# Layer norms by column thirds between the products, and feed-forward low parts behind the w_down additions

## Chip, cores and metric

The kernel runs on one core of one Trainium2 chip. The metric is device time in microseconds (us) of one launch, the median of several runs. Lower is better.

## The reference, cut to what matters

One inference step of a one-layer hybrid decoder (attention and a state-space branch in parallel). The change touches only its end, for TOK = 1056 tokens (1024 prompt, 32 sample) of 1024 features:

```
h = layer_norm(ALPHA * x + merged @ w_out, ln1_g, ln1_b)
y = layer_norm(ALPHA * h + (silu(h @ w_gate) * (h @ w_up)) @ w_down, ln2_g, ln2_b)
# layer_norm: (x - mean) * rsqrt(var + 1e-5) * g + b, mean and var over the 1024 features
```

Everything is in float32, inputs and outputs.

## The kernel before

Features lie on the 128 partitions (KT = 8 tiles of them), tokens along the free dimension. A product in float32 is made of three products of parts: each operand is split into a high part (fp32r, a rounded copy) and a low part (what is left), and TensorE (PE) adds high·high, high·low and low·high. One "unit" is 128 x 1024 weights; a dense unit makes one tile of 128 output features for all 1056 tokens: 8 tiles x 3 parts x 3 column thirds of CH = 352 tokens, 72 matmuls (`products`, L893). The three thirds of one output lie in three banks of PSUM (bank set 0 is banks 0 to 2, bank set 1 banks 3 to 5).

GpSimd (POOL) splits each unit of weights: `whi` (L736), then `wlo` (L738), into one of two slots, when PE has released that slot (`unit_done`). SyncE (SP) loads the raw weights four units ahead. VectorE (DVE) makes the low parts of activations and all additions, ScalarE (ACT) the high parts, SiLU, squares and roots.

The order of the work, written out by hand on each engine with semaphores:

1. w_out, eight dense units. For each tile DVE adds ALPHA * x (L2477) into `mm` and adds the tile into the running sum `srow` (L2470).
2. Layer norm 1 over all 1056 tokens at once: PE multiplies `srow` by a matrix of ones (L1386), which gives each partition the sum of the features; ACT makes the mean row `murow` (L1830); DVE subtracts it from eight tiles (L2487); ACT squares each tile (L1835) and PE adds the squares, again by the matrix of ones (24 matmuls of 352 columns); ACT takes the root (L1804), DVE the reciprocal over 128 x 1056 (L2496); then per tile DVE scales (L2492), ACT makes the high part `ahi` (L1842), DVE the low part `alo` (L2503).
3. Feed-forward in 11 blocks of 256 hidden features. A block has four dense units (gate and up for j = 0 and 1) and two w_down units. In the code order of PE: block n+1's gate and up, then block n's w_down. DVE: `hidden` makes the products silu(gate) * up into `ff` (L2516) for j = 0 and 1, then both low parts `flo` (L2519); then `down` adds eight outputs into `mm` (`add`, L2417), which frees the bank sets (`res_free0`, `res_free1`) for PE. The last block's w_down stands alone, its additions also make `srow`.
4. Layer norm 2 as in 2, but reciprocal, scaling and bias by thirds; PE turns the result by token (L1469), DVE and ACT each copy half of a tile into one of two buffers `ytok` (L2548, L1868), ACT issues the store.

The loop of DVE in the feed-forward stands in two functions:

```
def hidden(v):
    for j in range(2):
        ...  # product into ff[j]
    for j in range(2):
        ...  # flo[2v+j] = ff[j] - fhi[2v+j]
```

Of the kernel before, what the change touches and what calls it, by code (L numbers as in the profile page):

```python
# [7 lines left out]
F32 = mybir.dt.float32  # L8
# [7 lines left out]
P = 128  # L16
# [80 lines left out]
THIRDS = 96  # L97
LEAD = 6
# [49 lines left out]
def build(nc, a, o, stop=99, debug=None):  # L148
# [5 lines left out]
             "gt_full1": ("rope_full", 32), "tok_stored0": ("x_stored", 32), "tok_stored1": ("prep_full", 48),  # L154
# [3 lines left out]
             "f_hi": ("cw_ready", 2), "f_split": ("st_turned", 2), "bank_read0": ("vecs_ready", 2),  # L158
             "bank_read1": ("qn_hi", 3), "ssq_ready": ("sq_ready", 2), "ssq_used": ("sq_used", 2),
# [7 lines left out]
             "inv_ready": ("e_ready", 32), "n_ready": ("dm_ready", 36)}  # L167
# [257 lines left out]
    srow, sq2, murow, rsrow = ar("srow", [P, TOK]), ar("sq2", [P, 2, TOK]), ar("murow", [P, TOK]), ar("rsrow", [P, TOK])  # L425
    ar = Arena(low)
# [4 lines left out]
    ytok = [Arena(low + 9 * 4096 + b * 4096)(f"ytok{b}", [P, D_MODEL]) for b in range(2)]  # L431
# [19 lines left out]
    def _(sp):  # L451
# [269 lines left out]
        next_weights(2)  # L721

# [139 lines left out]
    def _(pe):  # L862
# [554 lines left out]
        for u in range(4):  # L1417
# [4 lines left out]
        def layer_norm():  # L1422

            pe.wait_ge(sem("srow_ready"), k["srow_ready"].next())
            pe.wait_ge(sem("res_free0"), k["res_free0"].next())
            ones_times(0, srow, True, True).then_inc(sem("mean_ready"), k["mean_ready"].adds(1))
            pe.wait_ge(sem("res_free1"), k["res_free1"].next())
            for e in range(KT):
                pe.wait_ge(sem("ssq_ready"), k["ssq_ready"].next())
                ones_times(1, sq2[:, e % 2], e == 0, e == KT - 1).then_inc(sem("ssq_used"), k["ssq_used"].adds(1))  # L1430

        layer_norm()


# [14 lines left out]
        gate_and_up(tile_split)  # L1449
# [5 lines left out]
        down(0)  # L1455
        layer_norm()

        thirds_done = 0
        for i in range(9):
            n = P if i < 8 else NS  # L1460
            if i == 0:
                for b in range(2):
                    pe.wait_ge(sem(f"res_free{b}"), k[f"res_free{b}"].next())
            pe.wait_ge(sem(f"bank_read{i % 2}"), k[f"bank_read{i % 2}"].held(2))
            while thirds_done * CH < i * P + n:
                pe.wait_ge(sem("affine_ready"), k["affine_ready"].next(KT))
                thirds_done += 1
            for e in range(KT):
                last = pe.transpose(ps[0:n, 2 * (i % 2) + e // 4, e % 4 * P:(e % 4 + 1) * P], mm[:, e, i * P:i * P + n], ident)  # L1469
            last.then_inc(sem("tok_turned"), k["tok_turned"].adds(1))  # L1470


    @block.scalar
    def _(act):
# [353 lines left out]
        def layer_norm():  # L1828
            act.wait_ge(sem("mean_ready"), k["mean_ready"].next())
            act.activation(thirds(murow[:, :]), out3(0), ACT.Copy, scale=1.0 / D_MODEL).then_inc(sem("res_free0"), k["res_free0"].adds(1))  # L1830
            for e in range(KT):
                act.wait_ge(sem("centred"), k["centred"].next())
                if e >= 2:
                    act.wait_ge(sem("ssq_used"), k["ssq_used"].next())
                act.activation(sq2[:, e % 2], mm[:, e], ACT.Square).then_inc(sem("ssq_ready"), k["ssq_ready"].adds(1))  # L1835
            act.wait_ge(sem("ssq_used"), k["ssq_used"].next(2))
            root(1, rsrow, D_MODEL)
        k["res_free1"].n += 6 * 4 + KT // 2
        layer_norm()
        for e in range(KT):  # L1840
            act.wait_ge(sem("scaled"), k["scaled"].next())
            act.activation(ahi[:, e], mm[:, e], ACT.Identity, bias=vecs[:, V_L1B + e:V_L1B + e + 1]).then_inc(sem("g_hi"), k["g_hi"].adds(1))  # L1842
# [9 lines left out]
        k["unit_done"].n = TOTAL_UNITS - 6 * NF  # L1852
        for j in range(2):
            gate(0, j)
# [6 lines left out]
        k["res_free1"].n += 4  # L1861
        layer_norm()
        def by_token(tiles):
            for i in tiles:
                n = P if i < 8 else NS
                act.wait_ge(sem("tok_turned"), k["tok_turned"].next())
                act.wait_ge(sem(f"tok_stored{i % 2}"), k[f"tok_stored{i % 2}"].same())
                act.activation(ytok[i % 2][0:n, 0:512], ps[0:n, 2 * (i % 2), :], ACT.Copy).then_inc(sem(f"bank_read{i % 2}"), k[f"bank_read{i % 2}"].adds(1))  # L1868
                k[f"bank_read{i % 2}"].n += 1
                act.wait_ge(sem(f"bank_read{i % 2}"), k[f"bank_read{i % 2}"].same())  # L1870
                dst = o["y_prompt"][0, i * P:i * P + n, :] if i < 8 else o["y_sample"].rearrange("b t d -> (b t) d")
                act.dma_start(dst, ytok[i % 2][0:n, :]).then_inc(sem(f"tok_stored{i % 2}"), k[f"tok_stored{i % 2}"].adds(16))
# [709 lines left out]
```

## Time and profile before

| | |
|---|---|
| median of 3 runs | 3094.28 us (3092.59 to 3104.74) |
| profiled execution, its own time | 3096.15 us |
| its span, first to last instruction | 3094.3 us |
| PE busy | 2908.1 us (94%) |
| DVE, ACT, POOL busy | 1556.8, 748.1, 1027.7 us |
| mean granted clock of PE | 0.966 |

The span is what the trace shows; 1.85 us of the execution's own time lie outside it. Times in the trace are counted from the start of the span. The granted clock is a share of PE's full speed: 1.00 is 2.4 GHz and 0.50 is 1.2 GHz. Ends of matmuls are modelled, so distances between starts are read rather than durations.

### The profile page before, as it was taken

What the parts mean: (1) busy time and instruction counts of PE and PEld (TensorE: products, weight loads), DVE (VectorE), ACT (ScalarE), POOL (GpSimd) and SP (SyncE); (2) the same over time, 40 slices, a digit from 0 to 9 for tenths busy, and PEclk for the clock granted to TensorE, in tenths of its full rate; (3) what the DMA queues carried; (4) which work ended last, traced back from release to release, by engine and by line L of the source; (5) the groups of instructions that cost most, each with busy time, mean ns of one, the idle gap of its engine ahead of it and who ended that gap; (6) DMA issues with size and microseconds to landing.
All of it is one profiled execution on the core that took longest, in us unless ns stands there. A gap on an engine that the chain in (4) does not pass through costs nothing.

```text
span 3094.3 us, 45505 instructions
## 1 busy us (share of the span) xinstructions
PE 2908.1 (94%) x18732; PEld 2591.8 (84%) x18732; DVE 1556.8 (50%) x2123; ACT 748.1 (24%) x1143; POOL 1027.7 (33%) x586
## 2 busy tenths in 40 slices
PE   7799999999999999999999688999799999999996
PEld 7789999999989975555776588999599999999995
DVE  2765787756474736554444567663512222222226
ACT  1211212435363624554332100100200000000003
POOL 3443333423232404544002032444133333333330
PEclk9899999999999979999999899999899999999998
DMA  4154234656564552223233323343011111111101
GB/s 134 54 162 138 83 100 136 161 158 162 165 171 132 155 148 62 65 82 139 101 147 138 112 91 119 126 153 103 22 48 42 45 45 42 42 48 42 42 21 56
DMA packets 314164, 308.84 MB, mean 100 GB/s; under 512 B 31813, under 2 KB 272714, under 8 KB 311498
## 3 DMA queue, kind: packets, MB, share of 16 engines
q1 hardware_dynamic: 250808, 190.24, 21.8%
q10 hardware_dynamic: 59594, 78.22, 7.3%
q0 software_dynamic: 3584, 37.75, 3.2%
q8 instruction: 143, 2.34, 0.3%
q14 instruction: 35, 0.29, 0.0%
HBM read 227.96 MB, written 78.20 MB: 99 GB/s over the span
## 4 chain that ended last, share of the span: by engine, by line
PE 69%; DVE 12%; issue 9%; POOL 5%; ACT 2%; DMA 2%; SPq 1%; ACTq 0%; POOLq 0%; DVEq 0%
PE ps L893 42%; PE ps L1053 10%; POOL pr L839 4%; PE ps L1386 2%; PE ps L1329 2%; PE ps L1289 2%; PE ps L1302 2%; DVE cv L2030 2%; DVE flo L2519 1%; PE ps L1306 1%; PE ps L1132 1%; PE ps L1086 1%; PE ps L1090 1%; PE ps L964 1%; PE ps L1079 1%
## 5 line engine op out<-in xcount | busy, mean ns | idle before, releaser
L736 POOL TENSOR_TENSOR whi<-raw,cst 128x1024 fp32r<-128x1024 f32 x160 | 309.0, 1931 | 1242.7 <-PE ps L893 1099.9
L893 PE MATMUL ps<-ahi,whi 128*128 128x352 f32 x1824 | 399.1, 327 | 54.7 <-DVE alo L2390 22.4
L738 POOL TENSOR_TENSOR wlo<-raw,whi 128x1024 fp32r<-128x1024 f32 x160 | 440.7, 2755 | 12.6
L893 PE MATMUL ps<-alo,whi 128*128 128x352 f32 x1824 | 397.3, 326 | 0.0
L893 PE MATMUL ps<-ahi,wlo 128*128 128x352 f32 x1824 | 393.7, 324 | 0.0
L893 PEld LDWEIGHTS ps<-ahi,whi 128*128 128x128 f32 x1824 | 311.7, 190 | 62.9 <-issue 40.0
L893 PEld LDWEIGHTS ps<-ahi,wlo 128*128 128x128 f32 x1824 | 313.8, 190 | 0.0
L893 PEld LDWEIGHTS ps<-alo,whi 128*128 128x128 f32 x1824 | 312.8, 189 | 0.0
L1053 PE MATMUL ps<-xhi,whi 128*128 128x352 f32 x768 | 256.0, 333 | 0.0
L1053 PE MATMUL ps<-xhi,wlo 128*128 128x352 f32 x768 | 248.0, 323 | 0.0
L1053 PE MATMUL ps<-xlo,whi 128*128 128x352 f32 x768 | 247.9, 323 | 0.0
L2417 DVE TENSOR_TENSOR mm<-ps,mm 128x1056 f32<-128x1056 f32 x112 | 139.7, 1256 | 151.2 <-PE ps L893 149.8
L839 POOL TENSOR_TENSOR pr<-pr,rowinv 128x384 f32<-128x384 f32 (+7 forms) x128 | 145.4, 1146 | 204.0 <-DVE rowinv L2235 203.0
L1183 PE MATMUL ps<-kb,qb 96*128 96x512 f32 (+3 forms) x384 | 161.2, 538 | 10.9 <-ACT pr L1704 8.4
L893 PE MATMUL ps<-xhi,whi 128*128 128x352 f32 x720 | 158.5, 329 | 6.7 <-ACT xraw L1570 4.4
L893 PE MATMUL ps<-xlo,whi 128*128 128x352 f32 x720 | 157.0, 326 | 0.0
L2228 DVE TENSOR_REDUCE rowmax<-ps 128x1 f32<-128x384 f32 (+7 forms) x128 | 97.0, 758 | 117.7 <-PE ps L1185 115.9
L893 PE MATMUL ps<-xhi,wlo 128*128 128x352 f32 x720 | 155.4, 324 | 0.0
L1183 PEld LDWEIGHTS ps<-kb,qb 96*128 96x128 f32 x384 | 65.5, 198 | 105.5 <-issue 77.0
L1053 PEld LDWEIGHTS ps<-xhi,whi 128*128 128x128 f32 x768 | 144.3, 188 | 7.9 <-issue 5.5
L1053 PEld LDWEIGHTS ps<-xlo,whi 128*128 128x128 f32 x768 | 144.4, 188 | 0.0
L1053 PEld LDWEIGHTS ps<-xhi,wlo 128*128 128x128 f32 x768 | 144.4, 188 | 0.0
(329 smaller groups left out, 5016.2 us busy)
## 6 DMA issues: line engine op xcount, KB each, us to landing
raw<-in_w_in SPq DMA_DIRECT2D x61, 512.0 KB, 5.1
s_a<-d_acum SPq DMA_DIRECT2D x32, 512.0 KB, 7.1
d_xbc<-so ACTq DMA_DIRECT2D x24, 528.0 KB, 2.7
gt<-d_g SPq DMA_DIRECT2D x24, 528.0 KB, 3.6
raw<-in_w_ffn_gate SPq DMA_DIRECT2D x22, 512.0 KB, 3.8
raw<-in_w_ffn_up SPq DMA_DIRECT2D x22, 512.0 KB, 3.8
raw<-in_w_ffn_down SPq DMA_DIRECT2D x22, 512.0 KB, 3.5
d_z<-zo ACTq DMA_DIRECT2D x16, 528.0 KB, 5.2
```

Of the source, the lines that this page charges most:

```text
L736: pool.tensor_tensor(whi[s][:, :], raw[:, u], ones[:, 0:1].broadcast_to([P, UNIT]), ALU.mult).then_inc(sem("unit_hi"), k["unit_hi"].adds(1))
L738: pool.tensor_tensor(wlo[s][:, :], raw[:, u], whi[s][:, :].bitcast(F32), ALU.subtract).then_inc(sem("unit_split"), k["unit_split"].adds(1))
L839: pool.tensor_tensor(pr[G][i][:, :], pr[G][i][:, :], rowinv[:, n:n + 1].broadcast_to([P, length]), ALU.mult).then_inc(sem("n_ready"), k["n ...
L893: last = pe.matmul(ps[0:m, 3 * b + c, 0:width], w(j), x[:, j, at:at + width], start=i == 0, stop=i == n - 1)
L1053: last = pe.matmul(ps[:, c, 0:CH], w[u % SPLIT][:, j * P:(j + 1) * P], x[:, j, c * CH:(c + 1) * CH], start=i == 0, stop=i == 3 * KT - 1)
L1183: pe.matmul(ps[:, first_bank + c // 512, 0:w], qb[pp][h][:, q * P:(q + 1) * P], kb[pp][h][:, c:c + w], start=True, stop=True)
L1289: last = pe.transpose(ps[:, 4 + i % 3, r * P:(r + 1) * P], src, ident)
L1302: pe.matmul(half(c, s), qcur[b][:, j, :], kvt[:, j, 4 * g:4 * g + 4, :].rearrange("p r n -> p (r n)"), start=j == 0, stop=False)
L1329: last = pe.matmul(ps[64 * s:64 * s + 64, 7, 0:KL], prt[:, i, 64 * s:64 * s + 64], kvb[b][:, 8 * c + 4 * s + i % 4, :], start=i == 0, stop ...
L1386: last = pe.matmul(ps[:, 3 * b + c, 0:width], ones, src[:, at:at + width], start=start, stop=stop_)
L2228: dve.tensor_reduce(rowmax[:, n:n + 1], src, AX, ALU.max).then_inc(step.sem, step.adds(1))
L2417: dve.tensor_tensor(thirds(mm[:, e]), out3(b), thirds(mm[:, e]), ALU.add).then_inc(sem(f"res_free{b}"), k[f"res_free{b}"].adds(1))
```

## The change

**Feed-forward.** In `hidden` the low part of j = 0 is made right behind the product of j = 0. The low part of j = 1 is made after the eight additions of `down` (and, at the end of the loop, the last w_down on PE still waits for it).

**Layer norms by thirds.** The sum, mean, centring, squares, root, factor, scaling and splitting are done for each third of 352 tokens. On PE they stand between products: the last two w_out units and the first two gate and up units go by thirds (`unit_third`), and the last w_down goes by thirds over the eight outputs (`last_down`), each part in the next of six banks.

**Statistics by token.** The sum of squares is no longer a product with the matrix of ones as the stationary operand. For each run of TS = 88 tokens the squares are the stationary operand (128 x 88) and one column of ones moves, so the sums of 88 tokens land in one column (32 matmuls a third, `square_sums`). The root and the reciprocal are then of 88 x 4 values, and `spread` brings them back to a row on all partitions (4 matmuls a third with the 88 x 88 identity moving); ACT copies that row to SBUF (`factor_row`). Centring and squaring take four tiles in one instruction (128 x 4 x 352).

**Output.** Nine buffers `ytok` in place of two, three pairs of banks in place of two, and SP issues the stores.

```diff
+        def square_sums(c, n):
+            pe.wait_ge(sem("row_read"), k["row_read"].held())
+            pe.wait_ge(sem("squared"), k["squared"].next(2))
+            for t in range(CH // TS):
+                for e in range(KT):
+                    last = pe.matmul(ps[0:TS, 7, CH + t:CH + t + 1], sqb[n][:, e, t * TS:(t + 1) * TS], ones[:, 0:1], start=e == 0, stop=e == KT - 1)
+            last.then_inc(sem("sums_done"), k["sums_done"].adds(1))
+        def spread(c):
+            pe.wait_ge(sem("inverted"), k["inverted"].next())
+            for t in range(CH // TS):
+                at = c * (CH // TS) + t
+                last = pe.matmul(ps[:, 7, t * TS:(t + 1) * TS], inv[0:TS, at:at + 1].broadcast_to([TS, P]), ident[0:TS, 0:TS], start=True, stop=True)
+            last.then_inc(sem("row_ready"), k["row_ready"].adds(1))
# PE, from w_out to the feed-forward
-        for u in range(4, 8):
-            dense(u, u % 2, ahi, alo, KT)
-        layer_norm()
+        unit_third(6, 0)
+        unit_third(7, 0)
+        unit_third(6, 1)
+        mean(0)
+        unit_third(7, 1)
+        unit_third(6, 2)
+        square_sums(0, 0)
+        mean(1)
+        unit_third(7, 2)
+        spread(0)
+        mean(2)
+        square_sums(1, 0)
+        unit_third(0, 0, "g_split")
+        spread(1)
+        unit_third(1, 0)
+        square_sums(2, 0)
+        unit_third(0, 1, "g_split")
+        spread(2)
+        unit_third(1, 1)
+        unit_third(0, 2, "g_split")
+        unit_third(1, 2)
+        for u in range(2, 4):
             dense(u, u % 2, ahi, alo, KT)
# PE, the end
+        pe.wait_ge(sem("f_split"), k["f_split"].next(2))
+        for b in range(2):
+            pe.wait_ge(sem(f"res_free{b}"), k[f"res_free{b}"].next())
+        last_down(0, 0, 8)
+        last_down(1, 0, 3)
+        mean(0)
+        last_down(1, 3, 8)
+        last_down(2, 0, 2)
+        mean(1)
+        last_down(2, 2, 3)
+        square_sums(0, 1)
+        last_down(2, 3, 6)
+        spread(0)
+        last_down(2, 6, 8)
+        mean(2)
+        square_sums(1, 1)
+        by_token(0)
+        by_token(1)
+        spread(1)
+        square_sums(2, 1)
+        spread(2)
+        for i in range(2, 9):
+            by_token(i)
# DVE, norm 1
+        last_residual(0)
+        centre(0)
+        last_residual(1)
+        inverse(0)
+        centre(1)
+        last_residual(2)
...
+        split_third(0)
+        inverse(1)
+        centre(2)
+        split_third(1)
+        inverse(2)
+        split_third(2)
# DVE, feed-forward
                 dve.tensor_tensor(thirds(ff[j][:, :]), out3(1), thirds(fg[j]), ALU.mult).then_inc(sem("res_free1"), k["res_free1"].adds(1))
-            for j in range(2):
-                dve.wait_ge(sem("f_hi"), k["f_hi"].next())
-                dve.tensor_tensor(flo[:, 2 * v + j], ff[j][:, :], fhi[:, 2 * v + j].bitcast(F32), ALU.subtract).then_inc(sem("f_split"), k["f_split"].adds(1))
+                if j == 0:
+                    low_part(v, 0)
...
             for v in range(2):
                 hidden(1 - v)
                 down()
+                low_part(1 - v, 1)
# DVE, the end: per part one addition into mm and one into srow
+        last_down(0, 0, 8)
+        last_down(1, 0, 3)
+        centre(0)
+        last_down(1, 3, 8)
+        last_down(2, 0, 2)
+        centre(1)
+        last_down(2, 2, 3)
+        inverse(0)
+        last_down(2, 3, 8)
+        scale_third(0)
+        centre(2)
+        inverse(1)
+        right_half(0)
+        right_half(1)
+        scale_third(1)
+        inverse(2)
+        right_half(2)
+        scale_third(2)
+        for i in range(3, 9):
+            right_half(i)
```

`last_residual(c)` is the ALPHA * x addition of tiles 6 and 7 for one third and their additions into `srow`; `centre(c)` two subtractions of 128 x 4 x 352; `split_third(c)` eight scalings and eight low parts of 352 columns, waiting for ACT's high parts; `low_part(v, j)` one `flo`. On ACT: mean row, squares, root, factor row, high parts or bias, for each third in turn.

## Rows read from the trace of the kernel before

**Rows 1.** The page, part 1: engine, busy time, share of the span, instructions.

```profile
PE 2908.1 (94%) x18732; PEld 2591.8 (84%) x18732; DVE 1556.8 (50%) x2123; ACT 748.1 (24%) x1143; POOL 1027.7 (33%) x586
```

**Rows 2.** Busy time of each engine by stretch, clock, DMA (norm 1, feed-forward, end).

```profile
core 0: us, PE busy (x) PEld busy (x) DVE busy (x) ACT busy (x) POOL busy (x), PEclk, DMA share, GB/s
2160.54:2252.95 92.41, 70.52 (x344) 60.16 (x343) 54.02 (x39) 22.61 (x20) 20.15 (x8) 0.87 0.12 35
2252.95:3009.68 756.73, 732.00 (x4465) 727.94 (x4464) 181.76 (x123) 46.10 (x43) 275.80 (x124) 0.99 0.14 42
3009.68:3094.30 84.62, 56.95 (x271) 47.37 (x269) 55.30 (x61) 29.45 (x44) 4.29 (x2) 0.86 0.13 52
```

**Rows 3.** Chain that ended last, around norm 1: start, length, what.

```profile
2186.88 3.90 PE ps L1386 x6
...
2194.40 17.05 PE ps L1386 x48
...
2212.65 6.76 DVE rsrow L2496
...
2238.12 24.00 PE ps L893 x147
```

**Rows 4.** Chain that ended last, at the end of the kernel.

```profile
3042.82 16.10 PE ps L1386 x48
...
3081.60 2.64 DMA out_y_prompt<-ytok
```

**Rows 5.** Waits from 2240 us on: who for whom, total, times, longest.

```profile
PE ps L893 <- DVE mm L2417: 21.3, 10, 2.2
```

**Rows 6.** PE in order of time, norm 1's gate unit, a w_down start: start, length, idle.

```profile
2233.20 0.75 PE L893 MATMUL ps<-ahi,whi 128*128 128x352 f32 x3 [0.75 <-DVE alo L2503]
2233.79 0.65 PE L893 MATMUL ps<-alo,whi 128*128 128x352 f32 x3
...
2987.15 0.65 PE L893 MATMUL ps<-flo,whi 128*128 128x352 f32 x3
2987.64 0.64 PE L893 MATMUL ps<-fhi,wlo 128*128 128x352 f32 x3
2990.44 0.75 PE L893 MATMUL ps<-fhi,whi 128*128 128x352 f32 x3 [2.17 <-DVE mm L2417]
...
2992.37 1.08 PE L893 MATMUL ps<-fhi,whi 128*128 128x352 f32 x3
2993.25 1.08 PE L893 MATMUL ps<-flo,whi 128*128 128x352 f32 x3
```

**Rows 7.** Line L2519, the low parts: least, median, greatest ns.

```profile
L2519 DVE TENSOR_TENSOR flo<-srow,fhi x11: 1719/1785/1879, 2277.4 to 2983.8; 128x1056 fp32r<-128x1056 f32 x11
L2519 DVE TENSOR_TENSOR flo<-rsrow,fhi x11: 3450/3455/3458, 2279.2 to 2985.5; 128x1056 fp32r<-128x1056 f32 x11
```

**Rows 8.** DVE and POOL in order of time at that w_down start.

```profile
2982.66 1.26 DVE L2516 TENSOR_TENSOR rsrow<-ps,sq 128x1056 f32<-128x1056 f32 x1 [21.89 <-PE ps L893]
...
2989.13 2.42 DVE L2417 TENSOR_TENSOR mm<-ps,mm 128x1056 f32<-128x1056 f32 x2
2982.61 1.89 POOL L736 TENSOR_TENSOR whi<-raw,cst 128x1024 fp32r<-128x1024 f32 x1 [7.26 <-PE ps L893]
2984.59 3.30 POOL L738 TENSOR_TENSOR wlo<-raw,whi 128x1024 fp32r<-128x1024 f32 x1
```

**Rows 9.** DVE and ACT in order of time, in the two norms.

```profile
2191.88 9.44 DVE L2487 TENSOR_TENSOR mm<-mm,murow 128x1056 f32<-128x1056 f32 x8 [5.06 <-ACT murow L1830]
3062.51 4.06 DVE L2492 SCALAR_TENSOR_TENSOR mm<-mm,vecs,rsrow 128x352 f32<-128x352 f32 x8
2198.36 1.08 ACT L1835 ACTIVATE sq<-mm 128x1056 f32<-128x1056 f32 x1 [2.93 <-PE ps L1386]
3063.12 4.06 ACT L1878 ACTIVATE mm<-mm,vecs 128x352 f32<-128x352 f32 x8 [3.04 <-DVE mm L2492]
```

**Rows 10.** PE in order of time, elsewhere: float32 matmuls with few moving columns.

```profile
1128.33 1.02 PE L1121 MATMUL ps<-s_e,s_it 128*64 128x4 f32 x16
...
1722.08 0.39 PE L1335 MATMUL ps<-rowsum,cst 128*128 128x5 f32 x2
1723.43 5.52 PE L1367 MATMUL ps<-cst,oseq 128*128 128x64 f32 x32 [0.97 <-DVE oseq L2339]
```

**Rows 11.** Busy time by stretch again: small matmuls, and turning by token.

```profile
1122.00:1127.00 5.00, 5.00 (x33) 4.10 (x32) 1.51 (x5) 1.16 (x2) 0.00 (x0) 0.50 0.86 225
3082.00:3084.00 2.00, 2.00 (x11) 2.00 (x10) 0.00 (x0) 0.60 (x1) 0.00 (x0) 0.50 0.81 322
3090.00:3092.00 2.00, 0.00 (x0) 0.00 (x0) 0.68 (x1) 0.59 (x1) 0.00 (x0) 1.00 0.99 395
```

More of the change, by code:

```diff
@@ L97 @@
 THIRDS = 96
+TS = 88
 LEAD = 6
@@ L1432, in _, with third, unit_third @@
-        layer_norm()
+        def third(c):
+            return slice(c * CH, (c + 1) * CH)
+        def unit_third(u, c, ready=None):
+            s = u % SPLIT
+            if c == 0:
+                pe.wait_ge(sem("unit_split"), k["unit_split"].next())
+                pe.wait_ge(sem(f"res_free{s}"), k[f"res_free{s}"].next())
+            for i in range(3 * KT):
+                j, part = divmod(i, 3)
+                if ready and part == 0:
+                    pe.wait_ge(sem(ready), k[ready].next())
+                w, x = ((whi, ahi), (whi, alo), (wlo, ahi))[part]
+                last = pe.matmul(ps[:, 3 * s + c, 0:CH], w[s][:, j * P:(j + 1) * P], x[:, j, third(c)], start=i == 0, stop=i == 3 * KT - 1)
+            last.then_inc(sem("unit_done" if c == 2 else "third_ok"), k["unit_done" if c == 2 else "third_ok"].adds(1))
@@ new lines, in mean @@
+        def mean(c):
+            pe.wait_ge(sem("srow_ready"), k["srow_ready"].next())
+            pe.wait_ge(sem("mu_ready"), k["mu_ready"].held())
+            pe.matmul(ps[:, 6, 0:CH], ones, srow[:, third(c)], start=True, stop=True).then_inc(sem("mean_ready"), k["mean_ready"].adds(1))
+        def square_sums(c, n):
[5 more added lines that the diff above has]
+            last.then_inc(sem("sums_done"), k["sums_done"].adds(1))
@@ L1838, in _, with squares @@
[L1838 to L1842, printed above, removed]
+            act.activation(murow[:, third(c)], ps[:, 6, 0:CH], ACT.Copy, scale=1.0 / D_MODEL).then_inc(sem("mu_ready"), k["mu_ready"].adds(1))
+        def squares(c, n):
+            for h in range(2):
+                act.wait_ge(sem("centred"), k["centred"].next())
+                if h == 0:
+                    act.wait_ge(sem("sums_done"), k["sums_done"].same())
+                act.activation(sqb[n][:, 4 * h:4 * h + 4, :], mm[:, 4 * h:4 * h + 4, third(c)], ACT.Square).then_inc(sem("squared"), k["squared"].adds(1))
@@ new lines, in high_parts @@
+        def high_parts(c):
+            for e in range(KT):
+                act.wait_ge(sem("scaled"), k["scaled"].next())
+                act.activation(ahi[:, e, third(c)], mm[:, e, third(c)], ACT.Identity, bias=vecs[:, V_L1B + e:V_L1B + e + 1]).then_inc(sem("g_hi"), k["g_hi"].adds(1))
+        mean_row(0)
+        squares(0, 0)
+        root_of(0)
+        mean_row(1)
+        squares(1, 0)
+        factor_row(0)
+        mean_row(2)
+        high_parts(0)
+        root_of(1)
+        factor_row(1)
@@ new lines, in centre, with inverse @@
+        def centre(c):
+            dve.wait_ge(sem("mu_ready"), k["mu_ready"].next())
+            dve.wait_ge(sem("srow_ready"), k["srow_ready"].same())
+            for h in range(2):
+                part = mm[:, 4 * h:4 * h + 4, third(c)]
+                dve.tensor_tensor(part, part, murow[:, third(c)].unsqueeze(1).broadcast_to([P, 4, CH]), ALU.subtract).then_inc(sem("centred"), k["centred"].adds(1))
+        def inverse(c):
+            n = CH // TS
+            dve.wait_ge(sem("rooted"), k["rooted"].next())
+            dve.reciprocal(inv[0:TS, c * n:(c + 1) * n], stat[0:TS, c * n:(c + 1) * n]).then_inc(sem("inverted"), k["inverted"].adds(1))
```

237 lines of the change are left out of this document (142 added, 95 removed).

## The prediction

> **What bounds the kernel.** I read the page's first part, then busy time by stretch, then the chain of waits and the timelines inside each stretch. PE is busy for 94% of the span [rows 1], so a stage is worth what PE loses in it. I cut the touched end of the kernel at three places of PE: the end of w_out unit 5 (2160.54), the end of the second feed-forward unit (2252.95), the start of the last w_down (3009.68). The stretches last 92.4, 756.7 and 84.6 us [rows 2].
>
> A product costs PE 0.485 us for three matmuls, start to start [rows 6]: 0.1616 each, 11.635 for a unit. The first stretch holds four units, 46.5 us, so norm 1 costs 45.9. The second holds 62 units (2, then 10 x 6), 721.4 us; 35.3 are lost. The third holds two, 23.3; norm 2 and the output cost 61.3.
>
> The chain in norm 1 [rows 3] is serial: sum on PE, 17.05 us of squares against ones, 6.76 of reciprocal, then scaling and splitting; PE runs freely only from 2238.12. Norm 2 repeats it [rows 4] and ends in stores. The loss in the feed-forward is PE waiting ten times for the first w_down addition, 21.3 us in all [rows 5]. After a wait of 2.17 us two groups run at 0.88 instead of 0.485 us [rows 6], half the clock; four such groups are 1.6 us. 2.1 + 1.6 = 3.7, and the stretch gives 3.53 per block.
>
> **Feed-forward low parts.** The first w_down addition starts at 2989.13 because two low parts, 1.78 and 3.45 us [rows 7], lie between it and the product at 2982.66 [rows 8]. Now only the product stands ahead: it ends at 2983.9. PE ends output 0 eighteen matmuls (2.91 us) after 2982.3, at 2985.2; the addition takes 1.26 and frees the bank set at 2986.5. PE wants it at 2988.1, so 1.6 us remain to spare. The low part of j = 0 moves into the 11.6 us before the second product; that of j = 1 follows the eighth addition, some 20 us before the next product. Both are hidden by PE's units, and without that cover would cost what they cost today. All 35.3 us go: **-35.3**. The tall low part is tall because of POOL: it starts under L738, which itself takes 3.30 then [rows 8].
>
> That row is what the Trainium skill states (SBUF — State Buffer, the section with the engine and AXI sides): a VectorE instruction with two SBUF inputs and a GpSimd one shut each other out for the whole instruction. The trace agrees, 3.45 us for what takes 1.2 otherwise.
>
> **Prices of the new operations.** *Square sums*, 32 matmuls, and the trace records a float32 matmul as two instructions: 64. Not seen in this shape. Lower bound from 64 stationary columns, 60 ns each (L1121, at half the clock), upper from 128 columns, 125 ns (L1335, start to start 0.13) [rows 10]: 3.8 to 8.0 us. 88 columns lie between, 84 ns in proportion: 5.4. *Spread*, 8 instructions with 128 stationary columns: L1367's 0.17 gives 1.3. *Mean*, three times a third of the 24 squares matmuls, 16.10/24 = 0.67 us [rows 4], at the full clock. *Centring*, 4 x 352 columns: 9.44/8 = 1.18 for 1056 [rows 9], so 1.57 each, 3.2 a third, unless the repeated row costs more (bound 2.5 each). *Squares* on ACT 1.08 x 4/3 = 1.4 each. *Small DVE or ACT operations* of 352 columns 0.51 [rows 9]; one that waits for the other's end 0.55. Root and inverse of 88 x 4: under 0.4 together with the handover. Three reciprocals of 2.3 and one of 6.76 go.
>
> The Trainium skill (TensorE: Matmul & The Clock Gate, the section on LDWEIGHTS) prices a load by its columns at P/1.2 ns. For 88 that is 73 ns; its estimate for a third's square sums would be 4.7 us. The 125 ns of 128 columns here is 107 and a little, so the trace agrees.
>
> **Norm 1**, from T = 0 at the end of unit 5. Unit 6 by thirds reaches 3.9. Unit 7 needs POOL's split of its slot, which starts at 0 and takes 1.89 + 3.30 [rows 8]: it starts at 5.4 (before, 11.6 us of unit 6 hid this) and its third ends at 9.3. Next third of unit 6: 13.2; mean: 13.9; third of 7, last third of 6: 21.6. Meanwhile centring ends at 17.7 and squares at 19.1, both in time. Square sums 27.0, mean 27.7, last third of unit 7 31.6, spread 32.9. Here DVE is late: centring of third 1 to 31.5, then four operations of the last residual to 33.8; mean(2) ends 34.5. Square sums 39.9. The gate unit follows DVE's splitting (16 operations, 8.2 us) to 43.8; spread 45.1, third of the up unit 48.9, square sums 54.4, gate third 58.2, spread 59.5, up third 63.4. The last gate third waits for DVE (scaling from 60.0, last low part 68.5): 69.0; last up third 72.9; the next unit waits for its split until 73.7.
>
> Two additions. The split of the up unit starts at 31.6, just where DVE's two additions into `srow` of third 2 have two SBUF inputs; by the 3.45 row one waits for L736 or L738: 0 to 3 us, I take 2. Clock: a wait of 2.17 costs 1.6 us behind it, one of 0.75 costs 0.1 [rows 6]; here are waits of 1.6 and 1 to 4, and PE stood at 0.50 under small matmuls though busy 5.00 of 5.00 us [rows 11], so the square sums may go with half the clock. Between none and five drops, 0 to 8; I take 2.5. Sum 78.2 against 92.4: **-14.2**. With square sums 3.8 and no additions 70 (-22); with 8.0 and 4 of additions 85.5 (-7).
>
> **The end**, from T = 0 at the start of the last w_down. A new wait: PE needs the last addition of the block before, and behind it on DVE the low part of j = 1: 1.3 + 1.8 (its start lies where the shorter one of rows 7 lies against POOL), so PE starts at 3.1; everything of that w_down stands behind this wait. From there DVE is slower than PE: a part costs PE 0.97, DVE two operations, 1.1. Sum of third 0 at 12.9; mean(1) waits 3.4 us for DVE and ends at 25.2; square sums 31.6; sum of third 2 at 39.1; scaling of third 0 43.2; square sums 45.2, tiles 0 and 1 47.3; spread 48.6; square sums 54.6; spread 56.6; tile 2 57.6. DVE's half of tile 2 (58.4) stands ahead of scaling of third 2, whose bias ends at 63.0. Six tiles are then turned; copies end at 67.8. Their stores, 2.75 MB at 0.395 MB per us [rows 11], outlast them: 72.2. Slow clock as in the turning now (0.50, [rows 11]), in the mean and the first parts: +4.3 (0 to 6). 76.5 against 84.6: **-8.1**; bounds -15 (3.8, no slow clock) and -2 (8.0, slow). Nine buffers remove the present waits for stores of 2.64 [rows 4]; SP is idle then, so its issue costs nothing.
>
> **Sum.** -35.3 - 14.2 - 8.1 = -57.6. The profiled execution's 3096.15 becomes 3038.5. Its time stands 1.87 above the median, 3094.28, so the forecast is **3037 us**.
>
> **Rivals.**
> - *The statistics are dear* (0.20): square sums near 8 us, or PE at half clock behind them. For: 125 ns with 128 columns and 0.50 under small matmuls. Against: the loads have 88 columns and dense work lies between. All bounds at the dear end: -35.3 - 7 - 2 = -44; with more drops -36. 3050 to 3058.
> - *Everything fits* (0.15): short square sums, no drop, no lock: -35.3 - 22 - 15 = -72: 3022.
> - *The feed-forward stall stays* (0.05), the change not doing what it says: another operation of DVE or ACT holds the bank set, and 1.6 us to spare are too few. Against: no such operation is in the queue. -22: 3072.
> - *Slower than before* (0.02): one mechanism, the price of a one-column float32 matmul. Each us more of square sums costs 3 us in each norm, so the gain is gone at 5.4 + 57.6/6 = 15 us, 235 ns an instruction, and 0.5% is lost at 17.6, 275 ns; at 18, 3112. Nothing in rows 10 is above 172.
>
> The forecast itself, 3029 to 3046, has 0.55; 0.03 lies elsewhere. The range from the bounds is 3022 to 3052: it leaves out half of the dear case, the stall and the slow one. Half a percent is 15.5 us, about what a measurement of this kernel can tell from no change: only the slow rival and part of the unnamed rest come near. Faster 0.95, same 0.03, slower 0.02.
>
> **What would show it.** No idle time of PE before the third output of w_down, and the middle stretch 721 to 723 us. First stretch 70 to 85, square sums 3.8 to 8.0 each, the clock behind them at 1.00. In the end, PE's first matmul of the last w_down about 3 us late, then DVE without pause. I am wrong if the clock is 0.50 for most of norm 1, if the 128 x 4 x 352 centring takes over 2.5 us, or if a stall comes back in the blocks.

## The result, and the profile after

The changed kernel takes 3063.22 us (median of 4 runs, 3053.06 to 3065.72) against 3094.7 for the kernel before on the same chip: a ratio of 0.9873, 95% interval 0.9853 to 0.9893. It is 31 us faster, where the forecast said 57; 3063 lies 11 us above the wide range of 3022 to 3052. The profiled execution took 3062.58 us, its span is 3060.8. The first part of the page, for [rows 1]:

```profile
PE 2922.0 (95%) x19068; PEld 2621.2 (86%) x19068; DVE 1562.5 (51%) x2190; ACT 753.1 (25%) x1169; POOL 1028.8 (34%) x586
```

Busy time by stretch of the changed kernel, cut where [rows 2] are cut (end of w_out unit 5, end of the second feed-forward unit, start of the last w_down); the number before the DMA share is the granted clock:

```profile
core 0: us, PE busy (x) PEld busy (x) DVE busy (x) ACT busy (x) POOL busy (x), PEclk, DMA share, GB/s
2169.23:2253.14 83.91, 78.54 (x510) 75.38 (x508) 53.17 (x75) 27.47 (x41) 18.84 (x9) 0.86 0.11 32
2253.14:2974.26 721.12, 721.12 (x4464) 720.83 (x4464) 184.53 (x127) 46.06 (x43) 274.72 (x124) 1.00 0.14 44
2974.26:3060.80 86.54, 71.86 (x439) 69.15 (x438) 53.29 (x89) 29.31 (x49) 5.14 (x2) 0.73 0.13 51
```

| stretch | before | forecast | after | after minus forecast |
|---|---|---|---|---|
| up to the end of unit 5 | 2160.54 | 2160.54 | 2169.23 | +8.7 |
| norm 1 | 92.4 | 78.2 | 83.9 | +5.7 |
| feed-forward | 756.7 | 721.4 | 721.1 | -0.3 |
| the end | 84.6 | 76.5 | 86.5 | +10.0 |

The last column sums to 24.1, and 3038.5 + 24.1 = 3062.6, the profiled execution's own time: nothing is missing. The feed-forward came as forecast, both norms are too long, and 8.7 us were lost where no line was changed. PE is busier than before in both norms (78.5 us against 70.5 in [rows 2], 71.9 against 57.0) and its clock at the end is 0.73 against 0.86: it waits less than before, and it is slow.

**Norm 1.** PE of the changed kernel in order of time (start, length, idle before): the mean, the square sums of the first third, the mean behind them, a product, then the square sums of the other two thirds.

```profile
2174.59 0.43 PE L1447 MATMUL ps<-ahi,whi 128*128 128x352 f32 x1 [1.59 <-POOL wlo L751]
2182.39 0.76 PE L1454 MATMUL ps<-srow,cst 128*128 128x352 f32 x2
...
2190.67 5.85 PE L1462 MATMUL ps<-cst,yz 128*88 128x1 f32 x64
2196.39 1.52 PE L1454 MATMUL ps<-srow,cst 128*128 128x352 f32 x2
2197.19 1.01 PE L1447 MATMUL ps<-ahi,whi 128*128 128x352 f32 x1
...
2206.60 7.83 PE L1462 MATMUL ps<-cst,yz 128*88 128x1 f32 x64
2214.29 0.64 PE L1447 MATMUL ps<-ahi,whi 128*128 128x352 f32 x1
```

The same stretches with the clock (the number behind the instruction count): sums, mean, product third; sums, product third; the last product third behind sums.

```profile
core 0: us, PE busy (x), PEclk, DMA share, GB/s
2190.78:2196.47 5.69, 5.69 (x66) 0.85 0.01 3
2196.47:2197.90 1.43, 1.43 (x4) 0.50 0.81 231
2197.94:2203.46 5.52, 5.52 (x26) 0.67 0.11 33
2206.70:2214.40 7.70, 7.70 (x66) 0.61 0.25 70
2214.40:2220.40 6.00, 6.00 (x28) 0.64 0.00 0
2230.90:2237.10 6.20, 6.20 (x27) 0.61 0.00 1
```

Up to the first square sums the ledger of the prediction holds to a tenth of a microsecond (with T = 0 at 2169.2: unit 7 at 5.4, mean at 13.2, square sums at 21.5). PE then goes from the full clock to the half clock while it is busy 5.69 of 5.69 us, and it stays low into the product behind. The three sums take 5.69 + 7.70 + 5.8 = 19.2 us (the third, at a clock of 0.83, isn't shown) where 16.2 stood in the ledger, and the three product thirds behind them 5.52 + 6.00 + 6.20 = 17.7 where 11.6 stood: 9.1 us, of a total of 10.2 over the ledger without its two additions. Those additions were 4.5, so 5.7 are left.

The clash of DVE and POOL that the prediction added is there, at the place it named. DVE of the changed kernel at the split of the up unit, which POOL starts at 2203.57:

```profile
2204.08 1.76 DVE L2636 TENSOR_TENSOR srow<-srow,mm 128x352 f32<-128x352 f32 x1
2205.77 3.16 DVE L2651 SCALAR_TENSOR_TENSOR mm<-mm,vecs,rsrow 128x352 f32<-128x352 f32 x2
```

The same operations take 0.52 and 0.58 each when POOL is quiet.

**The end.** PE of the changed kernel in order of time:

```profile
2977.47 0.66 PE L1530 MATMUL ps<-fhi,whi 128*128 128x352 f32 x1 [3.21 <-DVE flo L2685]
...
3000.26 1.50 PE L1454 MATMUL ps<-srow,cst 128*128 128x352 f32 x2 [1.99 <-DVE srow L2732]
...
3003.32 6.46 PE L1462 MATMUL ps<-cst,sqb 128*88 128x1 f32 x64
...
3019.81 7.93 PE L1462 MATMUL ps<-cst,sqb 128*88 128x1 f32 x59
3027.61 3.62 PE L1547 MATMUL ps<-cst,mm 128*128 128x128 f32 x16
...
3032.63 7.98 PE L1462 MATMUL ps<-cst,sqb 128*88 128x1 f32 x64 [0.55 <-ACT rsrow L1950]
3041.17 2.01 PE L1470 MATMUL ps<-cst,inv 88*128 88x88 f32 x8 [0.56 <-DVE inv L2648]
```

The wait of 3.1 us at the last w_down is 3.21. The sums take 6.5, 8.1 and 8.0 us (the second starts at 3019.47; its row above lacks its first instructions), 22.6 against 16.2. The first parts go at a clock of 0.50, the parts behind the first sums at 0.56, the turning at 0.65, and the last spread takes 2.01 us where the others take 1.02. The last copy ends at 3056.4, that is 82.1 after the start of the last w_down where the ledger had 67.8. The kernel ends 4.4 us behind it, and the ledger had 4.4 there too (72.2 less 67.8): the stores kept their share, and all else came later.

### The profile page after: what moved, and what is told of

It reads as the page before. It is cut to its first block, busy times and chain, and to the rows that moved or that the text cites. A ratio compares the mean times of both kernels' runs of the same rounds, so it can differ in the third digit from the quotient of the medians.

```text
span 3060.8 us, 46298 instructions
## 1 busy us (share of the span) xinstructions
PE 2922.0 (95%) x19068; PEld 2621.2 (86%) x19068; DVE 1562.5 (51%) x2190; ACT 753.1 (25%) x1169; POOL 1028.8 (34%) x586
## 4 chain that ended last, share of the span: by engine, by line
PE 68%; DVE 11%; issue 10%; POOL 5%; ACT 2%; DMA 2%; SPq 1%; ACTq 0%; POOLq 0%; DVEq 0%
PE ps L906 39%; PE ps L1066 10%; POOL pr L852 4%; DVE cv L2168 3%; PE ps L1342 2%; PE ps L1302 2%; PE ps L1315 2%; PE ps L1462 1%; PE ps L1447 1%; PE ps L1319 1%; DVE cv L2162 1%; PE ps L1145 1%; PE ps L1099 1%; DVE cv L2170 1%; DMA gt<-d_z 1%
## 5 line engine op out<-in xcount | busy, mean ns | idle before, releaser
L751 POOL TENSOR_TENSOR wlo<-raw,whi 128x1024 fp32r<-128x1024 f32 x160 | 438.8, 2742 | 12.6
L906 PE MATMUL ps<-ahi,whi 128*128 128x352 f32 x1728 | 377.1, 326 | 37.2 <-DVE alo L2528 21.8
L906 PE MATMUL ps<-alo,whi 128*128 128x352 f32 x1728 | 376.2, 326 | 0.0
L906 PE MATMUL ps<-ahi,wlo 128*128 128x352 f32 x1728 | 373.4, 325 | 0.0
L906 PEld LDWEIGHTS ps<-ahi,whi 128*128 128x128 f32 x1728 | 295.5, 190 | 42.8 <-issue 22.0
L906 PEld LDWEIGHTS ps<-ahi,wlo 128*128 128x128 f32 x1728 | 297.5, 190 | 0.0
L906 PEld LDWEIGHTS ps<-alo,whi 128*128 128x128 f32 x1728 | 296.1, 189 | 0.0
L2555 DVE TENSOR_TENSOR mm<-ps,mm 128x1056 f32<-128x1056 f32 x104 | 130.5, 1257 | 164.9 <-PE ps L906 164.8
```

The source lines that it names most:

```text
L751: pool.tensor_tensor(wlo[s][:, :], raw[:, u], whi[s][:, :].bitcast(F32), ALU.subtract).then_inc(sem("unit_split"), k["unit_split"].adds(1))
L906: last = pe.matmul(ps[0:m, 3 * b + c, 0:width], w(j), x[:, j, at:at + width], start=i == 0, stop=i == n - 1)
L2555: dve.tensor_tensor(thirds(mm[:, e]), out3(b), thirds(mm[:, e]), ALU.add).then_inc(sem(f"res_free{b}"), k[f"res_free{b}"].adds(1))
```

## The experiments

All kernels stand beside runs of the kernel before on the same chip. In the stages, "head" is the end of w_out unit 5; they are read from the starts of POOL's splits, which moves the cuts by up to 0.3 us against the windows above. Each row is one profiled execution; the median is of all runs.

| kernel | median, us | ratio, 95% | head | norm 1 | feed-forward | end |
|---|---|---|---|---|---|---|
| low parts only | 3073.7 | 0.9915 (0.9892 to 0.9939) | 2161.1 | 92.3 | 725.5 | 90.6 |
| old end | 3064.45 | 0.9888 (0.9867 to 0.9910) | 2160.5 | 84.2 | 720.9 | 92.0 |
| norms only | 3086.59 | 0.9948 (0.9929 to 0.9967) | 2166.1 | 84.2 | 750.8 | 82.6 |
| changed kernel again | 3058.83 | 0.9854 (0.9835 to 0.9874) | 2168.8 | 85.7 | 720.9 | 85.1 |
| sums twice | 3114.17 | 1.0048 (1.0031 to 1.0065) | 2163.0 | 111.9 | 726.0 | 110.9 |
| sums by ones | 3045.55 | 0.9821 (0.9805 to 0.9838) | 2167.0 | 78.5 | 724.6 | 73.9 |
| sums between | 3076.76 | 0.9922 (0.9897 to 0.9947) | 2166.0 | 101.0 | 720.9 | 86.5 |
| low part mid | 3057.56 | 0.9866 (0.9850 to 0.9883) | 2167.8 | 84.1 | 720.9 | 82.8 |
| ones and mid | 3044.62 | 0.9819 (0.9800 to 0.9838) | 2169.3 | 78.6 | 725.0 | 72.4 |
| kernel before again | 3103.86, one run | | 2169.2 | 91.1 | 757.2 | 84.5 |
| changed kernel once more | 3059.81, one run | | 2166.5 | 84.1 | 720.9 | 86.5 |

The kernel before had medians of 3102.81 us beside the first four kernels, 3101.21 beside the next four and 3100.47 beside the last three.

### The parts alone

**Low parts only.** The kernel before with the feed-forward part of the change; norms and output as before.

```diff
+        def low_part(v, j):
+            dve.wait_ge(sem("f_hi"), k["f_hi"].next())
+            dve.tensor_tensor(flo[:, 2 * v + j], ff[j][:, :], fhi[:, 2 * v + j].bitcast(F32), ALU.subtract).then_inc(sem("f_split"), k["f_split"].adds(1))
-            for j in range(2):
-                dve.wait_ge(sem("f_hi"), k["f_hi"].next())
-                dve.tensor_tensor(flo[:, 2 * v + j], ...)
+                if j == 0:
+                    low_part(v, 0)
...
+        low_part(0, 1)
...
+                low_part(1 - v, 1)
```

> The kernel before with the feed-forward low parts moved and nothing else. By the traces of before and after, the stretch of the blocks falls from 756.7 to 721.1 us (-35.6), norm 1 and the end stay at 92.4 and 84.6 us. Theory A (the unchanged part ahead of norm 1 varies from execution to execution by some 9 us, and the changed kernel's profiled execution was a long one): median near 3059, and the end of w_out unit 5 lies anywhere between 2160 and 2170 us in the trace. Theory B (the 8.7 us belong to the changed program's norm code): unit 5 ends at 2160.5 again and the median is 3059. Rival C (the low part behind the additions makes a stall elsewhere): more than 3065.

**Old end.** The changed kernel with the last w_down, layer norm 2 and the output of the kernel before (one `ps` bank set after the other, squares against ones, two `ytok`, stores from ACT). PE's part of the edit:

```diff
-        last_down(0, 0, 8)
-        last_down(1, 0, 3)
-        mean(0)
...
-        for i in range(2, 9):
-            by_token(i)
+        down(0)
+        layer_norm()
```

> The changed kernel with its end (last w_down, layer norm 2, output) as it was before: low parts moved, norm 1 by thirds, norm 2 over all tokens. By the traces: norm 1 stretch 83.9 us, blocks 721.1, end 84.6, which is 1.9 us less than the end by thirds. Expected 1 to 3 us faster than the changed kernel of the same chip, about 3051 if unit 5 ends at 2160 and 3060 if it ends at 2169. Rival: the end by thirds is worth the 8 us that were forecast and the profiled execution only hid it; then this kernel is 8 us slower than the changed one.

**Norms only.** The changed kernel with both low parts back ahead of the additions.

```diff
-                if j == 0:
-                    low_part(v, 0)
+            for j in range(2):
+                low_part(v, j)
...
-                low_part(1 - v, 1)
```

> The changed kernel with both low parts ahead of the w_down additions, as before: norms by thirds alone. By the traces: norm 1 stretch 83.9 (-8.5), blocks 756.7, end: the new wait for the low part of j = 1 goes, some 1.5 us of 86.5, so about 85 (+0.4). Expected -8 without the 8.7 us ahead of norm 1: 3087; if these belong to the program (theory B): 3095; if they vary (theory A): either, from run to run.

**The changed kernel again**, on the same chip.

> The changed kernel once more, for its profile and its times on the same chip. Theory A: unit 5 ends anywhere between 2160 and 2170 us, and the three stretches behind it are again 83.9, 721.1 and 86.5 us within 2 us each; the median lies between 3053 and 3063. Theory B: unit 5 ends at 2169 again.

Waits of PE in the blocks (total, times, longest): the kernel before beside its stalls of [rows 5], the norms-only kernel and the low-parts-only kernel, one fence each. "issue" is time in which PE waited for nothing that the profile shows.

```profile
PE ps L893 <- issue: 3.4, 4, 1.2
```

```profile
PE ps L906 <- DVE mm L2555: 21.3, 10, 2.2
```

```profile
PE ps L893 <- issue: 3.5, 4, 1.1
```

The norms-only kernel has the ten stalls of [rows 5] and no gaps: 750.8 - 720.9 = 29.9 us is what the stalls and the slow groups behind them cost, and it is all that the move of the low parts gives back. The clock doesn't fall behind each stall. Here are the 6 us of PE behind the second and the third stall of the kernel before:

```profile
2402.80:2408.80 6.00, 6.00 (x37) 1.00 0.11 33
2475.80:2481.80 6.00, 6.00 (x28) 0.72 0.10 29
```

Five of its ten stalls are like the second line, with nine matmuls fewer or some 1.5 us lost, and five like the first; in the norms-only kernel it is four and six. Waits of 21.3 us and five times 1.5 make 28.8 of the 35.3 lost in the kernel before; waits of 21.3 and four times 1.5 make 27.3 of the 29.9 in the norms-only kernel, and its other 2.6 us were not traced.

The low-parts-only kernel has no stall in the blocks but four small gaps in which PE waited for nothing shown, 0.7 to 1.1 us, 141 us apart, which is one pass of the loop (12 units, five passes): one at each jump back. Its blocks take 725.5, so the gaps and what stands behind them cost 4.6. The kernel before has both. The gaps go with the program and not with the low parts: both executions of the kernel before have them, and so do "sums twice" (4.2 us in four), "sums by ones" (2.7) and "ones and mid", two of which have the changed kernel's loop unchanged, while the changed kernel has none in three executions. What in a program makes them was not tried.

At the end, low parts only costs 90.6 - 84.6 = 6.0 us and old end 7.4: the new wait of 3.2 is in both traces, with a slow clock behind it and no gain beside them. So "low parts only" missed its expectation: 3073.7 is 29.1 below the kernel before on its chip, where a median near 3059 was expected. "Old end" missed too: 1 to 3 us less than the changed kernel was expected, and it takes 5.6 more (3064.45 against 3058.83 on the same chip; the ends are 92.0 and 85.1). The end by thirds is worth something then, but only against an old end that has the new wait as well. The norm-1 part is worth 8.2 us in "old end" and in "norms only" alike.

### The square sums

**Sums twice.** Each third's 32 one-column matmuls are made twice over.

```diff
-            for t in range(CH // TS):
+            for t in [*range(CH // TS)] * 2:
```

> The changed kernel with each square sum made twice, 64 one-column matmuls a third in place of 32 (the second writes the same sums). It measures what they cost on the path. By the prediction's ledger each us more in a third's sums costs 3 us in each norm: with 5.4 to 8 us a third, 32 to 48 us more in all. If DVE's chain hid part of them, less than 25; if the clock stays at half in the doubled run (8 us for 64 instructions), up to 50.

PE in order of time, the first two doubled sums:

```profile
2184.45 15.15 PE L1462 MATMUL ps<-cst,yz 128*88 128x1 f32 x128
...
2208.61 18.36 PE L1462 MATMUL ps<-cst,yz 128*88 128x1 f32 x128
```

Norm 1 grows by 26 to 28 us and the end by 24.4 to 25.8, 52 in all and some 9 us a third for 64 more instructions, each of which costs about 0.14 us. That is more than the 32 to 48 expected. The sums themselves grew by 9.3 to 10.5 us a third, so the prediction's slope (3 us in each norm for each us of a third's sums) roughly holds. So does its slower rival, which put the end of the gain at 15 us a third and a loss of 0.5% at 17.6: here are 15 to 18 us, and 3114.17 is 0.5% above the kernel before.

**Sums by ones.** By thirds as in the changed kernel, but the sum of squares is again a product with the matrix of ones (16 instructions with 352 moving columns), root and reciprocal over 128 x 352, and no spread.

```diff
-            for t in range(CH // TS):
-                for e in range(KT):
-                    last = pe.matmul(ps[0:TS, 7, CH + t:CH + t + 1], sqb[n][:, e, t * TS:(t + 1) * TS], ones[:, 0:1], start=e == 0, stop=e == KT - 1)
+            for e in range(KT):
+                last = pe.matmul(ps[:, 7, 0:CH], ones, sqb[n][:, e, :], start=e == 0, stop=e == KT - 1)
...
-        spread(0)
...
-            dve.reciprocal(inv[0:TS, c * n:(c + 1) * n], stat[0:TS, c * n:(c + 1) * n])...
+            dve.reciprocal(rsrow[:, third(c)], rsrow[:, third(c)])...
```

> The changed kernel with the square sums of both norms made as before, by the matrix of ones with 352 columns moving, still by thirds: 8 matmuls a third in place of 32 with one column, no spread, no factor row; DVE takes the reciprocal over 128 x 352 (2.35 us a third). Theory A (the one-column matmuls let the clock fall to half, inside them and in the products behind): a third's sums cost 8 x 0.59 = 4.7 us in place of 5.7 to 8.2, the clock of the products behind them is 1.00, and both stretches shrink: norm 1 from 84 to about 77 us, the end from 86 to about 78, some 12 us in all. Theory B (what makes the norms long is DVE's chain): the three reciprocals add 7 us to each stretch, and the kernel is as slow as the changed one or slower.

The three stretches of this kernel, and two of its sums in order of time:

```profile
2167.00:2245.50 78.50, 67.33 (x343) 57.45 (x342) 59.05 (x75) 27.06 (x38) 20.41 (x9) 0.96 0.12 34
2245.50:2970.10 724.60, 721.87 (x4464) 720.43 (x4463) 184.33 (x127) 46.06 (x43) 275.10 (x124) 1.00 0.15 44
2970.10:3044.00 73.90, 54.84 (x270) 46.06 (x270) 58.82 (x89) 28.94 (x46) 5.16 (x2) 0.87 0.15 59
```

```profile
2188.41 4.89 PE L1461 MATMUL ps<-yz,cst 128*128 128x352 f32 x16
...
2204.07 1.54 PE L1454 MATMUL ps<-srow,cst 128*128 128x352 f32 x2 [6.34 <-DVE srow L2614]
2205.40 7.00 PE L1461 MATMUL ps<-yz,cst 128*128 128x352 f32 x16
```

The same columns as above (clock behind the instruction count) for the first of these sums:

```profile
2188.30:2193.10 4.80, 4.80 (x18) 1.00 0.02 3
```

This is the kernel that settles the cause. Sums that move 352 columns leave the clock at 0.96 in norm 1 and 0.87 at the end, where one-column sums gave 0.86 and 0.73; the stretches are 78.5 and 73.9, the first what the forecast had for the changed kernel, the second less. DVE's three reciprocals and a wait of 6.3 us for DVE are in that price, and it still wins 5.4 to 7.2 and 11.2 to 12.6 us over the changed kernel's executions. The sums by ones also fall to half clock once, behind the wait of 6.34 (7.00 us instead of 4.89). The statistics by token are thus a loss here; the thirds are the gain. What of the one-column matmuls it is (one moving column in place of 352, or 88 stationary columns in place of 128) these runs don't separate, and the kernel without spread and factor row also has fewer handovers; what those gave back was not measured apart.

**Sums between.** The one-column matmuls of each third stand one or two behind every product matmul of the next third of products, so that they never form a row.

```diff
+        def with_sums(u, t, ready, c, n):
...
+            for i in range(3 * KT):
...
+                last = pe.matmul(ps[:, 3 * s + t, 0:CH], w[s][:, j * P:(j + 1) * P], x[:, j, third(t)], start=i == 0, stop=i == 3 * KT - 1)
+                for q in range(i * 32 // 24, (i + 1) * 32 // 24):
+                    r, e = divmod(q, KT)
+                    sums = pe.matmul(ps[0:TS, 7, CH + r:CH + r + 1], sqb[n][:, e, r * TS:(r + 1) * TS], ones[:, 0:1], start=e == 0, stop=e == KT - 1)
...
-        square_sums(0, 0)
         mean(1)
-        unit_third(7, 2)
+        with_sums(7, 2, None, 0, 0)
```

> The changed kernel with one thing moved: in norm 1 the 32 one-column matmuls of a third are not issued in a row but one or two behind each of the 24 matmuls of the product third beside them. Same instructions, same count. Theory A (a row of 64 one-column instructions lets the clock fall): the clock stays at 1.00 through norm 1, 24 products with 32 sums take 3.9 + at most 5.7 us in place of 5.7 + 5.6 or 7.7 + 6.0, so the PE time of the three pairs falls by some 6 to 8 us; DVE gets the sums later, so the stretch falls by 2 to 6 us from 84. Theory B (the clock falls for the gaps of PE, not for the one-column matmuls): clock as now, stretch as now or longer by the later sums.

Norm 1's first mixed stretch by clock, and PE where it falls:

```profile
2187.00:2194.70 7.70, 7.70 (x67) 1.00 0.15 42
2194.70:2215.00 20.30, 11.84 (x53) 0.50 0.12 36
```

```profile
2194.28 0.24 PE L1472 MATMUL ps<-cst,yz 128*88 128x1 f32 x2
2194.38 0.41 PE L1469 MATMUL ps<-alo,whi 128*128 128x352 f32 x1
2194.63 0.25 PE L1472 MATMUL ps<-cst,yz 128*88 128x1 f32 x2
2194.74 0.59 PE L1469 MATMUL ps<-ahi,wlo 128*128 128x352 f32 x1
2195.12 0.65 PE L1472 MATMUL ps<-cst,yz 128*88 128x1 f32 x4
```

The clock falls in the middle of the mixture, with PE busy all the time, and stays at 0.50. Waits stand in that second stretch, but the next mixture has none and is as slow:

```profile
2215.00:2225.40 10.40, 10.40 (x53) 0.50 0.01 2
```

Norm 1 takes 101.0 us, 15 to 17 more than with the sums in a row. The expectation had the row of 64 as the cause and a shorter stretch; it isn't the row that does it: small matmuls pull the clock down when they are spread among products too, and then the products beside them pay. Part of the 101.0 is a wait of 6.2 us of the last mean for DVE, which the later order brings; its share was not measured apart.

### The low part at the last w_down

**Low part mid.** The second low part between the third and the fourth of the eight additions.

```diff
                 add(e, e % 2)
+                if e == 2:
+                    low_part(v, 1)
...
-                low_part(1 - v, 1)
```

> The changed kernel with the low part of j = 1 between the third and the fourth w_down addition in place of behind the eighth. There DVE has 1.65 us to spare for 1.26 us and POOL is idle. Theory A (the low part behind the additions makes PE start the last w_down 3.2 us late and at half the clock): the blocks stay at 721 us, the last w_down starts at once, and the end falls from 85 to 86.5 us by 3 to 5. Rival (the wait for the last additions holds PE as long anyway, or DVE sets the end): the end falls by 1.5 us at most.

PE at its last w_down:

```profile
2974.34 0.40 PE L1530 MATMUL ps<-fhi,whi 128*128 128x352 f32 x1 [1.55 <-DVE mm L2555]
2974.57 0.32 PE L1530 MATMUL ps<-flo,whi 128*128 128x352 f32 x1
```

The wait is 1.55 us instead of 3.21, now for the last addition, and the matmuls behind it go at full clock (0.16 us from one to the next). The end takes 82.8 us, 2.3 to 3.7 less, and the blocks are as short as before. "Norms only", with the low parts ahead, has 82.6. In the whole time the gain doesn't show: the ratio is 0.9866 where the changed kernel has 0.9854 and 0.9873.

**Ones and mid.** Both in one kernel.

> Token sums by the ones matrix as in the kernel before, but by column thirds, and the second low part of w_down between the third and the fourth addition. If the small square-sum matmuls and the low part's place are two separate costs, they add: against the changed kernel -5.7 us in norm 1 and some -12 us at the end from the sums, some -3 us at the end from the low part's place. The end then measures about 71 us, norm 1's stretch 78.5, the blocks 720.9 or 724.6, and the whole 3038 to 3045 us. If instead the wait of 3.2 us at the last w_down is hidden behind DVE's other work once the sums are cheap, the end stays at 74 us and the whole at 3044.

3044.62 against 3045.55 of "sums by ones": the two can't be told apart, though the end measures 72.4 against 73.9. At the end 1.5 of the 3 us arrive; where the others go was not traced. Both are faster than either kernel of this case: their eight runs take 3040.69 to 3046.97 us, the nine of the changed kernel 3052.64 to 3065.72.

### The 8.7 us ahead of norm 1

**The kernel before again**, unchanged:

> The kernel before, unchanged, profiled once more. If the 5 to 9 us that the changed kernels lose ahead of norm 1 come from how DVE and POOL happen to fall against each other in one execution, the end of w_out's unit 5 comes here anywhere between 2160 and 2169 us; if they belong to the program, it comes at 2160.5 as in the first profile, and the four small gaps at the loop's jump back are there again.

**The changed kernel once more**:

> The changed kernel, unchanged, profiled a third time. If the loss ahead of norm 1 belongs to the program, the end of w_out's unit 5 comes at 2168.8 to 2169.2 us as twice before and the blocks take 720.9 us; if it is chance, elsewhere between 2160 and 2169.

The kernel before has its unit 5 end at 2160.54 in one profile and at 2169.2 in the other; the changed kernel at 2169.2, 2168.8 and 2166.5. The same program gives both, so it is no cost of the change. The two profiles of the kernel before may come from different chips, but on one chip the first four kernels of the table, edited only behind this point, lie between 2160.5 and 2168.8, and seven runs of the kernel before on one chip differ by 8 to 10 us. It is chance of the execution as far as these runs show. DVE by line from 510 to 582 us (the convolution, 15 operations of the same shape), first the kernel before in its first profile, then in its second:

```profile
L2030 DVE SCALAR_TENSOR_TENSOR cv<-xraw,cw,cv 128x1024 f32<-128x1024 f32 x15 | 19.3, 1285 | 0.5
```

```profile
L2030 DVE SCALAR_TENSOR_TENSOR cv<-xraw,cw,cv 128x1024 f32<-128x1024 f32 x15 | 23.1, 1543 | 0.5
L2024 DVE TENSOR_SCALAR cv<-xraw,cw 128x1024 f32<-128x1024 f32 x5 | 7.8, 1563 | 0.0
```

PE in that second profile, in order of time:

```profile
570.36 1.91 PE L1145 MATMUL ps<-cst,ccol 128*27 128x128 f32 x8 [4.78 <-DVE cv L2032]
```

In the first profile PE is busy all of the 71.5 us from 510 to 581.5, at the full clock. In the second it is busy for 65.7 of them: two of DVE's 15 operations start just behind a split of POOL and take 3.47 and 2.97 us, the convolution comes late, PE waits 4.78 us and goes at half the clock for a while. One such meeting, DVE and then POOL:

```profile
519.68 3.47 DVE L2030 SCALAR_TENSOR_TENSOR cv<-xraw,cw,cv 128x1024 f32<-128x1024 f32 x1
519.67 2.40 POOL L738 TENSOR_TENSOR wlo<-raw,whi 128x1024 fp32r<-128x1024 f32 x1
```

POOL's splits date the loss: the split at 551.35 in the first profile comes 0.9 us later in the second, the one at 580.24 comes 9.8 later, the one at 2089.83 comes 8.7 later. The changed kernel's first profile shows 23.1, 1542 for the same line, so the two are the same case.

## Why the prediction was right and wrong

**Right: the feed-forward, -35.3.** Measured -35.6, with PE busy 721.12 of 721.12 us; the 1.6 us to spare at the first addition held in all ten blocks. But the account of it was wrong in part, and the sum came right by luck. All 35.3 were given to the stall, as 2.1 + 1.6 a block; "norms only" shows 29.9 for it. The slow clock follows only half of the stalls, and [rows 6] shows one of that half. The rest goes with four issue gaps of 3.4 us in all, and the changed program happens to have none. They stand in the same view of waits as [rows 5], unpriced.

**Right: the places.** The wait of 3.1 at the last w_down (3.21), the clash of DVE and POOL in norm 1, the centring of 1.57 an instruction (3.16 for two), the spread of 1.3 (0.87 to 1.02 at the full clock, 2.01 at half) and the slope of 3.

**Wrong: the size of the square sums and of the clock behind them**, the two terms "88 columns lie between, 84 ns in proportion: 5.4" and "I take 2.5". Measured are 5.7, 7.7 and 5.8 us in norm 1 and 6.5, 8.1 and 8.0 at the end, against bounds of 3.8 to 8.0: all above 5.4, and three of six at the dear end. And the products behind each of them run at 0.61 to 0.67: 6.1 us in norm 1. The row that said so was [rows 11], 0.50 under small matmuls though PE was busy all of the 5.00 us. I took it as a possibility with a small weight, because dense work lay between; "sums between" shows that dense work does not protect. The first rival (0.20) was the right one, for this mechanism: it gave -44, and the stages measure -8.5 - 35.6 + 1.9 = -42.2. Its time, 3050 to 3058, was missed all the same, by the head (below).

By its load rate the Trainium skill (TensorE: Matmul & The Clock Gate, the section on LDWEIGHTS) gives an estimate of 4.7 us for a third's sums; the trace shows 5.69 at best, and no run shows these sums at the full clock throughout. The same page of the Trainium skill, in its section on HAM oscillation, ties the fall of the clock to idle gaps of PE. The trace shows that it also falls without one: PE was busy 5.69 of 5.69 us, and its last wait, 1.59 us, had ended 16 us earlier.

**Wrong: the end, -8.1, which became +1.9.** It is the same cause three times over, and a slow clock behind the new wait, which the low part's place brings (2.3 to 3.7 us by "low part mid"). There, less dense work lies between the sums, and "+4.3" for the slow clock stood for the mean and the first parts alone. The copies end 14.3 us behind the ledger without that term. The bound of -2 doesn't come out of the prediction's own terms either: 72.2 + 3 x 2.6 for sums of 8.0 us + 6 for the slow clock is 86.0, or +1.4, where 86.5 was measured. With sums by ones the end is 73.9: the order by thirds and the nine buffers were worth 10.7 us with the new wait paid, and the one-column sums with what belongs to them took 12.6 back.

**Not in the prediction: the head.** The sum started from the time of one profile, 2160.54, as if it were the kernel's own. The runs of the kernel before lie between 3092.59 and 3106.23 us, and the profiled one, 3096.15, was among the shorter. Against the medians of 3100 to 3103 measured beside the experiments, -57.6 would have meant 3043 to 3045, and the changed kernel took 3058.83: 14 to 16 too little gain, which is 5.7 + 10.0 - 0.3. The other 8.7 us are where the two profiles happened to fall. Beside its own baseline that run gains 44.0 us, and the range of 3022 to 3052 stands for gains of 42 to 72. So that 3063 lies so far outside is in good part this chance; that 57 was forecast and some 43 are there is the square sums and the clock.

## What to carry to other kernels

Price a matmul by what it does to the clock of its neighbours too: a formulation that moves one column at a time can be cheaper by its own count and dearer in the time, and if the trace shows half the clock under a busy PE anywhere, take that as the likely case wherever such matmuls are put. Before summing, list every wait of the stretch, those with no releaser too, see that the sum of causes gives the loss, and look at more than one of ten like stalls before its cost is multiplied by ten. When a kernel has engines that can shut each other out, look at the same cut in two profiles of the same kernel before a difference of a few microseconds ahead of the change is given a meaning.

## What was unexpected in the hardware

- A float32 matmul of one moving column with 88 stationary columns stands in the trace as two instructions, each about 0.09 us at a clock of 0.85 (64 in 5.69 us) and 0.12 at 0.61 (64 in 7.70); the 16 instructions with 352 moving columns that do the same sums take 4.75 us at 1.00.
- The dense products behind such sums pay too: a product third takes 5.5 to 6.2 us instead of 3.88, at a clock of 0.61 to 0.67.
- An unchanged kernel has two courses in the convolution, 8.7 us apart at the same cut, by how DVE's and POOL's operations happen to meet (1285 ns against 1543 ns in the mean for the same 15 operations).
- After the same wait of PE, 2.1 to 2.2 us, the clock falls to half in five of ten blocks and stays at 1.00 in the other five.
- PE pauses 0.6 to 1.2 us at each jump back of a loop in some programs and never in others with the same loop: 2.7 to 4.2 us a run, and 3.7 to 5.1 us of the feed-forward's time.
